# Three queues reordered in the up projection, the first visit and the gate tiles

## What is computed

```python
def second_block(x, p, ...):                       # x: 1 x 1024 tokens x 1024, p: 1 x 1024 x 256
    ...
        h = rms_norm(x, g_ffn_pre[l])
        up = h @ w_up[l]                                             # 1024 -> 2 x 3072
        gate_h = causal_dwconv(up[..., :D_FF], ffn_conv_w[l], ffn_conv_b[l])
        hid = jax.nn.gelu(gate_h) * up[..., D_FF:]
        x = x + rms_norm(hid @ w_down[l], g_ffn_post[l])             # 3072 -> 1024

        ple_gate = jax.nn.sigmoid(rms_norm(x, g_ple_gate[l]) @ w_ple_gate[l])
        ple = rms_norm(p[l].astype(x.dtype) @ w_ple_proj[l], g_ple_post[l])
        x = x + ple_gate * ple
    return x
```

## Time and profile before

| | |
|---|---|
| median of three runs | 3237.39 us (3234.96 to 3240.34) |
| profiled execution | 3240.55 us, span 3238.8 us, mean granted TensorE clock 0.978 |
| busy, share of the span | PE 94%, PEld 75%, DVE 76%, ACT 48%, POOL 29% |
| chain that ended last | PE 52%, DVE 7%, SP's queue 4%, DMA 2%, ACT 1% |
| up projection, block pair 3 | from 2446.3 us |
| down projection | visit 0 from 2836.1 us, the last visit to 3085.1 us |
| gate, first row to last tile | 3113.8 to 3227.6 us |

### The profile page before, as it was taken

How to read it: one execution, slowest core, us unless ns; L and a number is a source line. 1 busy time by engine, 2 the same in 40 slices (tenths; PEclk the granted TensorE clock), 3 DMA queues, 4 the chain that set the end, 5 groups by cost and what they waited for, 6 DMA issues and landing times.

```text
span 3238.8 us, 45088 instructions
## 1 busy us (share of the span) xinstructions
PE 3052.0 (94%) x14741; PEld 2432.0 (75%) x14741; DVE 2470.0 (76%) x3225; ACT 1561.4 (48%) x2154; POOL 952.9 (29%) x523
## 2 busy tenths in 40 slices
PE   6999999888998699999969999999999999989998
PEld 5668776666787588888857888888767888878767
DVE  7788867787554899999966776633398888898876
ACT  4345433667312688888852166311263333444352
POOL 2223332000242111111103433345414444434322
PEclk8999999999999799999989999999999999999999
DMA  7213221341241999999973122133223332454412
GB/s 266 72 53 105 59 72 52 101 121 42 64 167 54 372 379 380 377 381 382 379 271 101 52 84 97 46 111 116 80 98 98 114 109 97 149 175 151 164 63 72
DMA packets 364514, 495.88 MB, mean 153 GB/s; under 512 B 35630, under 2 KB 226012, under 8 KB 364388
## 3 DMA queue, kind: packets, MB, share of 16 engines
q1 hardware_dynamic: 349588, 459.61, 41.5%
q10 hardware_dynamic: 5440, 17.86, 1.7%
q0 software_dynamic: 9360, 16.80, 1.4%
HBM read 424.93 MB, written 80.77 MB: 156 GB/s over the span
## 4 chain that ended last, share of the span: by engine, by line
PE 52%; DVE 7%; SPq 4%; DMA 2%; issue 2%; ACT 1%; POOL 0%; DVEq 0%; ACTq 0%; POOLq 0%
PE acc L449 6%; PE acc L451 6%; PE acc L450 6%; PE acc L2048 3%; PE acc L2049 3%; PE acc L2050 3%; PE acc L3540 2%; PE acc L3542 2%; PE acc L3541 2%; SPq L1951 1%; PE acc L2067 1%; PE acc L2069 1%; PE acc L2068 1%; PE Y L3540 1%; PE Y L3542 1%
## 5 line engine op out<-in xcount | busy, mean ns | idle before, releaser
L422 POOL TENSOR_TENSOR whi<-wraw,one 128x1024 fp32r<-128x1024 f32 (+1 forms) x129 | 244.4, 1894 | 1167.2 <-PE acc L451 881.1
L449 PE MATMUL acc<-Ah,whi 128*128 128x512 f32 x1344 | 533.9, 397 | 1.5 <-DVE Al L1547 0.9
L451 PE MATMUL acc<-Ah,wlo 128*128 128x512 f32 x1344 | 525.1, 391 | 0.0
L450 PE MATMUL acc<-Al,whi 128*128 128x512 f32 x1344 | 524.9, 391 | 0.0
L2161 DVE TENSOR_TENSOR mlo<-mraw,mhi 128x1024 fp32r<-128x1024 f32 x256 | 307.1, 1223 | 38.2 <-ACT mhi L2105 25.1
L424 POOL TENSOR_TENSOR wlo<-wraw,whi 128x1024 fp32r<-128x1024 f32 (+1 forms) x129 | 319.2, 2474 | 10.1
L449 PEld LDWEIGHTS acc<-Ah,whi 128*128 128x128 f32 x1344 | 252.7, 188 | 69.0 <-issue 15.3
L2105 ACT ACTIVATE mhi<-mraw 128x1024 fp32r<-128x1024 f32 x256 | 268.0, 1063 | 75.0 <-PE acc L2050 53.0
L450 PEld LDWEIGHTS acc<-Al,whi 128*128 128x128 f32 x1344 | 252.8, 188 | 55.1 <-issue 3.1
L451 PEld LDWEIGHTS acc<-Ah,wlo 128*128 128x128 f32 x1344 | 252.6, 188 | 54.3
L2048 PE MATMUL acc<-mhi,XTh 128*128 128x512 f32 x512 | 204.1, 399 | 3.5 <-DVE XTl L2156 3.5
(11 more groups left out here) (819 smaller groups left out, 7425.3 us busy)
## 6 DMA issues: line engine op xcount, KB each, us to landing
mraw<-in_exp_w SPq DMA_DIRECT2D x512, 256.0 KB
mraw<-in_exp_w SPq DMA_DIRECT2D x128, 512.0 KB, 11.8
wraw<-in_w_in SPq DMA_DIRECT2D x72, 512.0 KB, 3.9
TT<-in_ada_w SPq DMA_DIRECT2D x32, 512.0 KB, 3.8
TT<-gates SPq DMA_DIRECT2D x32, 512.0 KB, 4.5
wraw<-in_w_up SPq DMA_DIRECT2D x44, 256.0 KB, 3.7
C<-in_w_up SPq DMA_DIRECT2D x44, 256.0 KB, 3.8
hidS<-TS SPq DMA_DIRECT2D x12, 768.0 KB, 4.3
```

The costliest lines, as they stand in the source:

```text
L422: ch(pool.tensor_tensor(hi[:, r, 0:k, 0:m], wraw[:, r, 0:k, 0:m], one[:, 0:1].unsqueeze(2).broadcast_to([P, k, m]), ALU.mult))
L449: pe.matmul(o, hi[:, hr, j, 0:m], ih[:, k0 + j, cols], start=(j == 0), stop=False)
L450: pe.matmul(o, hi[:, hr, j, 0:m], il[:, k0 + j, cols], start=False, stop=False)
L451: last = pe.matmul(o, lo[:, hr, j, 0:m], ih[:, k0 + j, cols], start=False, stop=(j == k - 1))
```

## The change

Five edits:

1. Pair 3 is peeled like pair 2 (`early_pair`), with three sums of hidden rows where pair 2 has one beside `bottom_rest`. On ACT its first copy stands ahead of `conv_first` (in pair 2 as well).
2. In visit 0 the first two sums of DVE stand between lows 3 and 4 instead of behind low 6.
3. SP issues the loads of the embedding rows as soon as part 0 of the last visit is done, ahead of the weights.
4. PE takes gate tiles 0 and 1 in turn: row j of tile 0, its mean, and from row 3 on row j - 3 of tile 1; then tile 1's last three rows. The mean of the embedding's norm goes from behind tile 2 into tile 3, behind its fourth row.
5. DVE makes the last five square sums behind `gate_raw(1)` instead of three before it and two behind.

```diff
@@ -2970,16 +2970,19 @@
             act.activation(up1[p], UBANKS[p][0], ACT.Copy).then_inc(S("u_p1"), 1)
 
         def pair(n, p, land=None, stored=None, first=False):
+            if first:
+                first_copy(n, p)
             conv_first(act, n, 1 - p, stored)
-            first_copy(n, p)
+            if not first:
+                first_copy(n, p)
             if land is not None:
                 act.wait_ge(S(f"uraw{1 - p}"), land)
                 weight_high(act, n + 1, 0, 1 - p)
             gelu(act, n, 1 - p)
             weight_high(act, n + 1, 1, 1 - p)
             if first:
-                act.wait_ge(S("u_mid"), 6 + 3)
-                act.wait_ge(S("second_row"), 2)
+                act.wait_ge(S("u_mid"), 3 * n + 3)
+                act.wait_ge(S("second_row"), n)
                 act.activation(uu[:, hi_tok], uf, ACT.Copy).then_inc(S("u_copied"), 1)
             if land is not None:
                 for i in range(2, 7):
@@ -3003,7 +3006,7 @@
         for i in range(3, 7):
             weight_high(act, 2, i, 0)
         pair(2, 0, 128, 64, True)
-        pair(3, 1, 128, 64)
+        pair(3, 1, 128, 64, True)
         with act.Fori(1, (BLOCKS - 2) // 2) as i:
             for r in range(2):
                 pair(2 * i + 2 + r, r, 64 * i + 128, 32 * i + 64)
@@ -3272,28 +3275,35 @@
             scaled_12()
             result_21(n, p)
 
-        result_e(2, 0)
-        result_f(2, 0)
-        dve.wait_ge(S("u_mid"), 6 + 2)
-        dve.wait_ge(S("u_used"), 14 + 4)
-        dve.tensor_tensor(uf, UBANKS[0][3], uf, ALU.add).then_inc(S("u_mid"), 1)
-        bottom_rest()
-        conv(2, 1)
-        weight_low(dve, 3, 0, 1)
-        weight_low(dve, 3, 1, 1)
-        second_half(2, 1)
-        dve.sem_inc(S("second_row"), 1)
-        weight_low(dve, 3, 2, 1)
-        weight_low(dve, 3, 3, 1)
-        result_11(2, 0)
-        weight_low(dve, 3, 4, 1)
-        top_sum()
-        result_12(2, 0)
-        weight_low(dve, 3, 5, 1)
-        scaled_12()
-        result_21(2, 0)
-        dve.wait_ge(S("u_copied"), 4)
-        pair(3, 1)
+        def early_pair(n, p):
+            result_e(n, p)
+            result_f(n, p)
+            dve.wait_ge(S("u_mid"), 3 * n + 2)
+            dve.wait_ge(S("u_used"), 7 * n + 4)
+            dve.tensor_tensor(uf, UBANKS[p][3], uf, ALU.add).then_inc(S("u_mid"), 1)
+            if n == 2:
+                bottom_rest()
+            conv(n, 1 - p)
+            weight_low(dve, n + 1, 0, 1 - p)
+            weight_low(dve, n + 1, 1, 1 - p)
+            second_half(n, 1 - p)
+            dve.sem_inc(S("second_row"), 1)
+            weight_low(dve, n + 1, 2, 1 - p)
+            weight_low(dve, n + 1, 3, 1 - p)
+            result_11(n, p)
+            weight_low(dve, n + 1, 4, 1 - p)
+            if p:
+                bottom_sums(hidden(1)[:, hi_tok])
+            else:
+                top_sum()
+            result_12(n, p)
+            weight_low(dve, n + 1, 5, 1 - p)
+            scaled_12()
+            result_21(n, p)
+            dve.wait_ge(S("u_copied"), n + 2)
+
+        early_pair(2, 0)
+        early_pair(3, 1)
         with dve.Fori(1, (BLOCKS - 2) // 2) as i:
             ch.enter(i - 1, 18)
             for r in range(2):
@@ -3335,7 +3345,7 @@
         x_first_low(0)
         down_low(n + 1, 5)
         result_21(n, 0)
-        for i in range(1, 7):
+        for i in range(1, 4):
             x_first_low(i)
 
         E_sum = (TT[:, 2, lo_tok], TT[:, 2, hi_tok], TT[:, 0, lo_tok], TT[:, 0, hi_tok])
@@ -3371,6 +3381,9 @@
             dve.wait_ge(S("u_used"), 7 * n + 2)
             add_to(e, b, False)
             dve.sem_inc(S("u_mid"), 1)
+            if v == 0:
+                for i in range(4, 7):
+                    x_first_low(i)
             if v:
                 x_low(v, 5)
                 x_low(v, 6)
@@ -3511,6 +3524,10 @@
                 sp.dma_start(window(i, 1, v % 4).bitcast(F32), window_source(i, j, j + 1)).then_inc(S(f"x_in{i}"), 16)
             if v == 1:
                 hid_store(sp, UP_PAIRS - 1, 0)
+        sp.wait_ge(S("u_used"), LAST + 1)
+        p_rows = A["p_2"][0, 0].rearrange("(b s p) n -> p b s n", p=P, s=2)
+        for r in range(2):
+            sp.dma_start(PR[:, :, r * 256:r * 256 + 256], p_rows[:, :, r, :]).then_inc(S("p_in"), 16)
         sp.wait_ge(S("u_lo"), 6 * (VISIT0 + VISITS - 1) + 6)
         sp.wait_ge(S("u_last_lo"), VISIT0 + VISITS)
         for t in range(2):
@@ -3521,10 +3538,6 @@
         def residual(b):
             sp.dma_start(X3[:, b, :], x3T[b * P:(b + 1) * P, :]).then_inc(S("x3T_in"), 16)
         residual(7)
-        sp.wait_ge(S("u_used"), LAST + 1)
-        p_rows = A["p_2"][0, 0].rearrange("(b s p) n -> p b s n", p=P, s=2)
-        for r in range(2):
-            sp.dma_start(PR[:, :, r * 256:r * 256 + 256], p_rows[:, :, r, :]).then_inc(S("p_in"), 16)
         for i, rows in ((2, (0,)), (3, (4,)), (4, (1,)), (5, (5,)), (6, (2,)), (7, (3, 6))):
             sp.wait_ge(S("u_used"), LAST + i)
             for b in rows:
@@ -3691,13 +3704,40 @@
             embedded(m)
 
         pe.wait_ge(S("n6_root_used"), 1)
-        product(pe, N0["pleg"], 0, Bh, Bl, free=take(0), ready=(S("n7_lo"), 0), after=square_mean)
-        for m in range(1, KD):
-            product(pe, N0["pleg"] + m, m % 2, Bh, Bl, free=take(m % 2))
-            if m == 2:
+        BEHIND = 3
+
+        def gate_rows(r, j):
+            for h in range(2):
+                o = acc[r][:, h * HALF:(h + 1) * HALF]
+                cols = slice(h * HALF, (h + 1) * HALF)
+                pe.matmul(o, whi[:, r, j, :], Bh[:, j, cols], start=(j == 0), stop=False)
+                pe.matmul(o, whi[:, r, j, :], Bl[:, j, cols], start=False, stop=False)
+                last = pe.matmul(o, wlo[:, r, j, :], Bh[:, j, cols], start=False, stop=(j == KD - 1))
+            if j == KD - 1:
+                last.then_inc(w_used, 1)
+
+        pe.wait_ge(w_lo, N0["pleg"] + 1)
+        pe.wait_ge(acc_free[0], take(0))
+        for j in range(KD):
+            pe.wait_ge(S("n7_lo"), j + 1)
+            gate_rows(0, j)
+            square_mean(j)
+            if j == BEHIND:
+                pe.wait_ge(w_lo, N0["pleg"] + 2)
+                pe.wait_ge(acc_free[1], take(1))
+            if j >= BEHIND:
+                gate_rows(1, j - BEHIND)
+        for j in range(KD - BEHIND, KD):
+            gate_rows(1, j)
+
+        def mean8(j):
+            if j == 3:
                 pe.wait_ge(S("n8_sum"), 1)
                 pe.wait_ge(S("n7_root_used"), 1)
                 add_mean(pe, S8, True, True, "n8_mean")
+
+        for m in range(2, KD):
+            product(pe, N0["pleg"] + m, m % 2, Bh, Bl, free=take(m % 2), after=mean8 if m == 3 else None)
             for t in TURNS[m]:
                 turn(t)
 
@@ -3814,10 +3854,8 @@
         newton_step(dve, ch, "n7", R7, TT[:, 2, :])
         dve.sem_inc(S("n7_root_used"), 1)
         gate_raw(0)
-        for p in (3, 4, 5):
-            square_sum(p)
         gate_raw(1)
-        for p in (6, 7):
+        for p in range(3, 8):
             square_sum(p)
         dve.sem_inc(S("n8_sum"), 1)
         gate_raw(2)
```

## The result

The changed kernel takes **3244.47 us** (median of 16 runs, 3241.87 to 3247.73) against 3236.58 (16 runs, 3232.20 to 3241.23) of the kernel before in the same rounds: a ratio of 1.0024, 95% interval 1.0017 to 1.0031, so 5.5 to 10.0 us slower. The forecast was 3243.5.

A forecast was written before the change was run, and what follows sets the result against it. PE carries half of the chain of waits, so edits pay only where PE stands still. Terms 1.0 + 1.3 - 2.2 + 6.0 = +6.1 us gave 3243.5 against the median of 3237.4; range 3232 to 3249.

The forecast's parts named there:

- B: Visit 0, two copies ahead of three lows: part 5 stays behind DVE's copy and meets slow matmuls; +1.3 us (0 to +1.7).
- C: Embedding rows loaded sooner: PE's 4.52 us wait goes, but DVE limits the gain; -2.2 us (-3.9 to -2).
- A: Pair 3 in the early order: its stall moves to pair 4 and is not removed; +1.0 us (-1 to +3).
- D: Gate tiles in turn: rows 4.6 us apart, first mean 3.6 later, embedding mean 6.1 to 7.7 later; +6.0 us (+4.2 to +9).
- The edit changes the order in this list, not the list: Visit 0: DVE's list has no idle time, so the copy at 2859.82 and PE's part 5 stay where they are.
- PE will again have idled 2.5 us before it: Norm's mean behind the embedding rows: idle PE may again bring the half clock (1.73 us), so no gain counted.
- one such op less, -1.9: Gate, behind the embedding's mean: the shifted DVE chain may meet one op fewer slowed by POOL's splits; -1.9 us.
- +1.7: Gate: PE idles before tiles 2 and 5 and may fall to the half clock; +1.7 us.
- The first two rivals: Peel is kept, pair 4 doesn't stall: 3235.0, chance 0.15. Gate tiles pay, PE's queue sets the end: 3235.0, chance 0.10.
- The dear end: Third rival, everything dear: clock drops before tiles 2 and 5, another in pair 4; typically +9, 3246.5 us, chance 0.22.

The follow-up runs named there:

- the second trace of the changed kernel: The changed kernel, with all five edits, run once more without further change to get another trace: 3243.46 us.

## Why the prediction was right

The forecast, 3243.5, is 1.0 us from the median. As a change it was +6.1 us, against 7.9 by the runs (5.5 to 10.0) and 6.6 by the stretches. Each stall was found where it was put; one step of B and one of C were wrong, and the errors in size nearly cancel, which is luck. Term by term:

- **A (+1.0, measured +1.4).** Right, with its times to 0.3 us. In times of the trace of before (1.5 us added, since after ran ahead by that much): e, f and the third sum done at 2459.8 (2459.5 forecast), the convolution of pair 4 from 2478.9 (2476.4 to 2478.6), its part 5 at 2486.1 (2484.7 to 2487.6). The waits of pair 4 were to be about 2 us before part 4 and 3 to 4 before part 5, and were 2.89 and 2.24. The two added sums took 1.67 and 1.66 us; 1.8 by the rows was near. Waiting for whole ops of POOL, as the rule of the Trainium skill has it (SBUF — State Buffer, Who interferes with whom), would have given about 2.0 us each by the prediction's estimate, too much by 0.3. Peeling two more pairs moved the stall again, to the first pair that is not peeled.
- **B (+1.3, measured +2.7).** Outside its own range (0 to +1.7): the half clock was mis-sized, and one step was wrong. The half clock behind part 5 was priced at up to 1.7 and taken at 1.3; it came in whole, since part 5 took 4.35, 5.05 and 4.37 us in the three traces with the edit. That is 1.7 us over the mean of the eight traces without the edit. The other 1.0 is the start of part 5. "The edit changes the order in this list, not the list", so the copy should have stayed; over the traces it came 1.0 us later against the visit's start (24.4 to 25.3 us, against 23.3 to 24.5 without it). The trace of before had the latest part 5 of the eight without the edit (24.53), so it hid this. The list is the same, but not its length: which of its ops run beside POOL's sums, and so take longer, changes. The seven lows and the two ops of the convolution take 21.1 to 21.8 us together in the eight traces without the edit, and 21.6, 22.1 and 22.6 in the three with it; the longest is the second trace of the changed kernel (4.48 us for the convolution, 2.60 in before). A weight part among them, short in two of the eight (0.68 us instead of 1.79) and in none of the three, makes up the rest. No run moved POOL's sums to try this.
- **C (-2.2, measured -2.4).** The main step is right: DVE's square sum and add close up, and PE's wait moves to the next product. That the size fits is in part luck. Of the 2.4 us, 1.5 lie between the last visit's start and the mean (36.3 us on average without the edit, 34.8 with it), and 0.9 behind, for which no gain had been counted: the leg from the mean to the first gate row took 18.1 to 18.2 us in all four traces with the edit, but also in four of the nine without it (19.6 to 19.9 in the rest). The step that failed is "PE will again have idled 2.5 us before it": PE idles at most 0.3 us before the mean in the four traces, 2.2 to 2.6 in the nine. Whether that keeps the mean at full clock (1.98 us in after instead of 3.50), these traces can't say, since four of the nine had it too.
- **D (+6.0, measured +4.9).** The mechanism held in every step: rows at 4.49 us (4.6 forecast), last mean +3.4 in the two first traces (3.6), tile 2 behind DVE's read of tile 0's bank with about 2.5 us of wait, embedding mean +6.1 (6.1 to 7.7). The term that was mis-sized is the correction behind the mean: "one such op less, -1.9" was let cancel against "+1.7" of the clock. The first came in all three traces. The second (2.5 us in two places) came only in one: behind the wait before tile 5 the clock halved in all three, but in after what PE lost was covered, since ACT's copy for the third transposition ended at 3203.8 and the transposition started at 3204.08. That transposition no longer waits, as it did for 1.53 us in before; DVE's chain now reaches PE at tile 5's bank.

The two errors, +1.4 on B and -1.1 on D, nearly cancel. The first two rivals fell: the peel wasn't kept, and the gate tiles didn't pay since PE's queue doesn't set the end there. The dear end (typically +9) is not ruled out by the runs, whose interval reaches 10.0; the stretches say 6.6. Pieces of it did come: a second half clock in pair 4, which cost nothing, and in the second trace of the changed kernel one behind tile 2 and a longer one behind tile 5 (2.5 us).

## What to carry to other kernels

Before a second stream of work is put into waits, measure the wait in each slot: 0.50 us per row took half a row's matmuls with a gain and a whole row's with none, since the engine became the slow one and the chain behind it moved. Removing a stall by a new order in a prologue is worth something only if the steady state can take over from it; otherwise it appears at the first iteration in the usual order. And a small edit is read from its own stretch over several traces, not from the totals of two.
